# The even mixer's low halves shared with GpSimd, and five start times of steps, in a two-model fp32 block kernel

## The reference, cut to what matters

```python
aq, ak = rms_norm(a_q, qk_gains[0]), rms_norm(a_k, qk_gains[1])      # 8 heads of 64
logf = log_sigmoid(a_f + f_bias); cum_logf = cumsum(logf)
a_out = softmax(aq ak^T * scale + cum_logf_i - cum_logf_j, causal) av # forgetting attention
b_out = (softmax(q1 k1^T) - lam * softmax(q2 k2^T)) bv                # 4 differential heads
out = concat(a_out, rms_norm(b_out, gain)) @ w_out
# cross attention: k = rms_norm(mem_n @ w_k) per head of 256, v = mem_n @ w_v
```

## Time and profile before

| | |
|---|---|
| median of 3 runs | 1910.07 us (1909.57 to 1913.3) |
| the profiled execution | 1915.36 us, its span 1913.5 us |
| PE busy | 1885.3 us (99%) |
| DVE busy | 1301.3 us (68%) |
| ACT busy | 1119.2 us (58%) |
| POOL busy | 331.9 us (17%) |
| chain that ended last | PE 84%, DVE 7%, ACT 4%, DMA 3% |

### The profile page before, as it was taken

The page is one execution under the profiler, slowest core; times in us unless marked ns, Lnnn a source line. Parts: engine busy times, 40 slices in busy tenths (PEclk is TensorE's granted clock), DMA queues, the critical chain, the costliest instruction groups (busy, mean ns, idle before and its releaser), DMA issues.

```text
span 1913.5 us, 24906 instructions
## 1 busy us (share of the span) xinstructions
PE 1885.3 (99%) x9073; PEld 1627.2 (85%) x9073; DVE 1301.3 (68%) x1919; ACT 1119.2 (58%) x1685; POOL 331.9 (17%) x559
## 2 busy tenths in 40 slices
PE   8999999999999999999999899999999999999999
PEld 7888888888888888888887788888888887788888
DVE  6687776666876775666578766776666577856664
ACT  5586555555866654655467565654555466665552
POOL 1110123111101531022100000431122011101220
PEclk9999999999999999999999999999999999999999
DMA  8866699878657997698865354997788787746884
GB/s 268 255 204 186 203 256 295 261 223 255 201 182 221 281 286 230 184 263 254 236 183 177 121 187 135 288 278 231 229 256 255 227 256 229 211 138 194 253 254 143
DMA packets 283497, 429.97 MB, mean 225 GB/s; under 512 B 25028, under 2 KB 161440, under 8 KB 283120
## 3 DMA queue, kind: packets, MB, share of 16 engines
q1 hardware_dynamic: 256144, 352.41, 60.3%
q0 software_dynamic: 26768, 75.64, 14.6%
q10 hardware_dynamic: 464, 0.34, 0.1%
HBM read 393.15 MB, written 35.15 MB: 224 GB/s over the span
## 4 chain that ended last, share of the span: by engine, by line
PE 84%; DVE 7%; ACT 4%; DMA 3%; issue 2%; POOL 0%; ACTq 0%; DVEq 0%; POOLq 0%
PE M L954 26%; PE M L956 26%; PE M L955 26%; DVE WL L1478 3%; ACT WH L1216 1%; PE AUX L998 1%; PE AUX L1185 1%; PE AUX L1163 1%; DMA TG<-squares 1%; DMA squares<-TG 1%; DVE SM L1664 1%; ACT TMP L1251 1%; DVE TMP L1621 0%; DMA SQI<-squares 0%; DMA RAW<-in_w_in 0%
## 5 line engine op out<-in xcount | busy, mean ns | idle before, releaser
L1478 DVE TENSOR_TENSOR WL<-RAW,WH 128x1024 fp32r<-128x1024 f32 (+1 forms) x670 | 811.1, 1215 | 460.0 <-ACT WH L1216 457.4
L1216 ACT ACTIVATE WH<-RAW 128x1024 fp32r<-128x1024 f32 (+1 forms) x670 | 703.6, 1054 | 525.4 <-PE M L956 475.6
L954 PE MATMUL M<-WH,Bh 128*128 128x512 f32 x1792 | 689.2, 385 | 3.4 <-DVE WL L1478 2.0
L955 PE MATMUL M<-WL,Bh 128*128 128x512 f32 x1792 | 679.7, 379 | 0.0
L956 PE MATMUL M<-WH,Bl 128*128 128x512 f32 x1792 | 679.7, 379 | 0.0
L954 PEld LDWEIGHTS M<-WH,Bh 128*128 128x128 f32 x1792 | 339.1, 189 | 53.1 <-DVE WL L1478 4.4
L956 PEld LDWEIGHTS M<-WH,Bl 128*128 128x128 f32 x1792 | 339.0, 189 | 48.0
L955 PEld LDWEIGHTS M<-WL,Bh 128*128 128x128 f32 x1792 | 339.2, 189 | 45.6
L1246 ACT ACTIVATE AS<-M,KEEP 128x256 f32<-128x256 f32 x132 | 55.4, 470 | 78.0 <-PE M L956 78.0
L954 PE MATMUL M<-WH,MTh 128*128 128x512 f32 x128 | 54.5, 426 | 0.0
L1893 POOL TENSOR_TENSOR KEEP<-SM,KEEP 128x2 f32<-128x2 f32 x15 | 10.7, 711 | 240.2 <-DVE SM L1532 240.1
(11 more groups left out here) (473 smaller groups left out, 2746.0 us busy)
## 6 DMA issues: line engine op xcount, KB each, us to landing
RAW<-in_ffn_w_in SPq DMA_DIRECT2D x352, 256.0 KB, 3.9
RAW<-in_w_in SPq DMA_DIRECT2D x103, 512.0 KB, 4.8
RAW<-in_w_gate_up SPq DMA_DIRECT2D x176, 256.0 KB, 4.6
RAW<-in_ffn_w_out SPq DMA_DIRECT2D x88, 512.0 KB, 4.7
RAW<-in_w_down SPq DMA_DIRECT2D x44, 512.0 KB, 4.8
RAW<-in_x_w_kv SPq DMA_DIRECT2D x32, 512.0 KB, 4.2
RAW<-in_even_w_in SPq DMA_DIRECT2D x24, 512.0 KB, 4.4
RAW<-in_odd_w_in SPq DMA_DIRECT2D x24, 512.0 KB, 5.1
```

The source lines that it names most:

```text
L954: e.matmul(out, s.hi, wh, start=s.at0, stop=False)
L955: e.matmul(out, s.hi, wl, start=False, stop=False)
L1216: e.activation(p.WH[:, h, 0:s.size], p.RAW[:, i, 0:s.size], ACT.Copy).then_inc(k.w_hi, 1)
L1478: e.tensor_tensor(p.WL[:, h, 0:s.size], p.RAW[:, s.u % NRAW, 0:s.size], hi.bitcast(F32), ALU.subtract).then_inc(k.w_lo, 1)
```

## The change

Units 352, 355, ... 391 of the weights (number modulo 3 is 1, conversion planned while `crowded` is set, which is while the even mixer and the projections behind it are planned) get their low half from GpSimd, with a semaphore of their own, `w_spare`. TensorE and SyncE wait for the semaphore that belongs to the unit (`low_made`). Apart from that, due times change: of the squares and norm of the first X (`late`), of rsqrt, product and exchange of the memory keys' norms where they have `room` (+5.0; the keys of heads 2 and 3 in layer 0, all four heads' keys in layer 1), of the transposes of `ak` (6.9 to 6.2), of the first suffix sum and the first pair's output in each layer of the first model, and of the forgetting heads of the even mixer (start 0.4 to 1.3 behind av, 2.75 to 2.65 between heads). In `b` the third case is 6.4 either way, as before.

```diff
+        self.lows, self.spare, n = [], set(), [0, 0]
+        for s in [s for s in steps if s.kind == "conv"]:
+            n[s.spare] += 1
+            self.lows.append((s.spare, n[s.spare]))
...
+            v.spare = self.crowded and v.u % 3 == 1
...
-        late = 4.5 if source == "load" else 0.0
+        late = 2.0 if source == "load" else 0.0
...
-        r = self.rsqrt(c.end + 3.2, s.v, n, s)
-        f = self.add("hn", c.end + 3.8)
+        wait = 5.0 if room is not None and groups == 2 else 0.0
+        r = self.rsqrt(c.end + 3.2 + wait, s.v, n, s)
+        f = self.add("hn", c.end + 3.8 + wait)
...
-            self.heads_out(c.end + 7.0, c.end + 21.0, "hn", f, s.xs, *room, lab, form, dst, gain)
+            self.heads_out(c.end + 7.0 + wait, c.end + 21.0 + wait, "hn", f, s.xs, *room, lab, form, dst, gain)
...
-        b = (c.end + (6.9 if lab in ("aq", "ak") else 6.4), 1.0) if finish[3] is None else (c.end + 7.6, 2.5)
+        b = (c.end + (6.9 if lab == "aq" else 6.2 if lab == "ak" else 6.4 if n < 8 else 6.4), 1.0) if finish[3] is None else (c.end + 7.6, 2.5)
...
-                q = self.add("st_s", b + (4.9 if i else 6.1))
+                q = self.add("st_s", b + (4.9 if i else 6.6))
...
-            o = self.add("st_o", b + 8.5)
+            o = self.add("st_o", b + (8.5 if hp else 9.0))
...
-        self.heads(c.end + 0.4, 2.75, lab_o, ["aq0", "aq1", "ak0", "ak1"], VA, QA, KA, av, S["NB"], A, 0.0)
+        self.heads(c.end + 1.3, 2.65, lab_o, ["aq0", "aq1", "ak0", "ak1"], VA, QA, KA, av, S["NB"], A, 0.0)
...
+def low_made(k, u):
+
+    spare, n = k.p.lows[u]
+    return (k.w_spare if spare else k.w_lo), n
...
-                e.wait_ge(k.w_lo, s.u + 1)
+                e.wait_ge(*low_made(k, s.u))
...
+        if s.kind == "conv" and s.spare:
+            continue
...
+        elif s.kind == "conv" and s.spare:
+            h = s.u % NHL
+            e.wait_ge(k.w_hi, s.u + 1)
+            hi = p.WH[:, h, 0:s.size]
+            e.tensor_tensor(p.WL[:, h, 0:s.size], p.RAW[:, s.u % NRAW, 0:s.size], hi.bitcast(F32), ALU.subtract).then_inc(k.w_spare, 1)
...
-            e.wait_ge(k.w_lo, i - NRAW + 1)
+            e.wait_ge(*low_made(k, i - NRAW))
...
+            p.crowded = l == 0
...
+            p.crowded = False
```

More of the change, by code:

```diff
@@ L232, in __init__ @@
         self.n_unit = self.n_conv = 0
+        self.crowded = False
         self.bank_use = [0] * 4
@@ L273, in order @@
                 busy[b] = s.at + s.late + HELD.get(s.kind, 1.5)
+        self.lows, self.spare, n = [], set(), [0, 0]
+        for s in [s for s in steps if s.kind == "conv"]:
+            n[s.spare] += 1
+            self.lows.append((s.spare, n[s.spare]))
+            if s.spare:
+                self.spare.add(s.u)
         for i, s in enumerate([s for s in dve if s.kind == "bt"]):
@@ L875, in __init__ @@
         self.raw = [sem(f"raw{i}") for i in range(NRAW)]
-        self.w_hi, self.w_lo, self.w_used = sem("w_hi"), sem("w_lo"), sem("w_used")
+        self.w_hi, self.w_lo, self.w_spare, self.w_used = sem("w_hi"), sem("w_lo"), sem("w_spare"), sem("w_used")
         self.m_out = [sem(f"m_out{i}") for i in range(4)]
```

## The result

The changed kernel took **1924.86 us** (median of 4 runs, 1923.84 to 1927.92), the kernel before in the same rounds 1911.1 us (1909.57 to 1913.3): ratio 1.0075, interval 1.0063 to 1.0088. It is 14 us slower where 1903 was forecast. The profiled execution took 1927.92 us, span 1926.1. Ratios are of undisturbed executions: one of the six of experiment 11 took 3312.57 us at a granted clock of 0.557 and is left out of its ratio.

What follows compares the result with a forecast made beforehand. TensorE, busy 99% of the span, was taken as the bound. Terms -2.1 - 1.3 - 1.1 - 2.7 + 1.4 = -5.8 us, with 1.5 of 5.1 us slow clock, took the median 1910.07 to 1903 us; range 1898 to 1909.

Steps and rivals of the forecast that it cites:

- the step on the subtractions: 14 low halves on GpSimd, 2.4 us each, half lost on VectorE: 0 net, bounds -2.1 to +3.6 and 1.1 lost again.
- rival 2: VectorE is held for the whole of each subtraction: +3.6 us, 1.1 back, slow clock kept, 1909 us; chance 0.17.
- the sum of the due times: Gains of start, output, ak and memory keys: -2.1, -1.3, -1.1 and -2.7 us, plus 5.1 us of slow clock.
- Start: Squares and norm of the first X earlier: TensorE's wait for a low half near 34 us goes, -2.1 us.
- Suffix sums and output: First suffix sum moved, 0; first heads' output one step back fills its wait at 131 us, twice, -1.3 us.
- Key turn and forget scores: Even mixer near 1053 us: a 1.6 us wait replaces the 2.65 us KA wait, -1.1 us; 3.4 slow clock goes.
- the wait behind the BO norm: Even mixer at 1069.56 us: TensorE's 0.58 us wait behind this norm moves and stays.
- Norm of memory keys: Even mixer at 1100 us: TensorE's 3.0 us wait shrinks, -2.7 us and 1.7 of slow clock; odd mixer 0.
- Queue of GpSimd: Unit 361 behind the forget rows delays unit 365 and the KB copy near 1010 us: +1.4 us, bounds 0 to +3.
- Clock: One slow stretch left in the mixers, at 1640 us, instead of three; 5.1 us of slow clock goes, 1.5 counted.
- Rival 3: The stops only move; only start and output count, -3.4 + 1.4: 1908 us; chance 0.08.
- Rival 4: GpSimd becomes the even mixer's bound if a subtraction takes over 3.2 us: 1916 us at 4.0, about 1930 at 5.4; chance 0.08.

Runs made afterwards that it cites:

- experiment 11: The changed kernel again, unaltered, beside the kernel before: 1926.62 us median, ratio 1.0077.
- experiment 12: Kernel before with three edits: start's squares and norm earlier, key turn of ak earlier, memory keys' norm later in the even mixer only: 1904.41 us, ratio 0.9962.
- experiment 8: Changed kernel with unit 361's low half back on VectorE, 13 left on GpSimd: 1925.02 us, ratio 1.0067 to the kernel before.
- experiment 3: Kernel before with only the squares and norm of the first X due earlier (2.0 for 4.5): 1908.74 us, ratio 0.9983.
- experiment 6: Kernel before with only the first suffix sum (6.6) and first pair's output (9.0) later, in both layers: 1914.07 us, ratio 1.0014.
- experiment 5: Kernel before with only the memory keys' norms 5.0 later, in both mixers: 1911.12 us, ratio 0.9993.
- Experiment 10: Kernel before plus four GpSimd memsets of 128x512 into an idle tile at each of the 14 units: 1911.67 us, ratio 0.9996.
- experiment 2: Kernel before with only the 14 subtractions moved to GpSimd: 1924.43 us, ratio 1.0065.
- experiment 7: Kernel before plus two GpSimd subtractions of a constant tile (128x512) into an unread tile at each of the 14 units: 1919.09 us, ratio 1.0039.

## Why the prediction was wrong

**The step that failed** is the one on the subtractions: "I take half of its 2.4 us as lost on VectorE, which is what it saves: 0". Alone they cost 12.6 us. The length was right (2.37 us undisturbed). Two things in the step were wrong. A hold lasts to the end of the subtraction, 1.9 to 2.4 us in nine of eleven, not half of it, which is what rival 2 said. And the sum was made as a balance of VectorE's time, 1.22 saved against 1.2 or 2.4 lost, with only three of 14 counted. The two sides of that balance aren't the same goods. The saving lies on a low half that is made 8 to 16 us ahead of its use. The hold falls on whatever VectorE does at that moment, here products for which TensorE stands waiting. It should have been priced like this, an estimate: number of subtractions that start beside a head product, times 2 us, nothing off for the saving. The rows at hand didn't say how many have slack behind them, but 14 times 2 us less some slack would have put the far end of the range beyond +10, not at +3.6. Rival 2 had the mechanism, with a chance of 0.17 and a price of +3.6; it was 12.6.

**A second step failed beside it**: the sum of the due times, -7.2 us and 5.1 of slow clock. Without the subtractions it came to nothing (1911.58 us, ratio 1.0002), which is outside the range of 1898 to 1909 as well. The terms follow below.

The Trainium skill (SBUF — State Buffer, section on SBUF's two separate sides) says that whichever of the two engines starts first has the shared ports for its whole instruction, against VectorE instructions with two SBUF inputs or in a fast mode, the former only if GpSimd reads SBUF. The runs agree. A held instruction ends soon behind GpSimd's: up to 0.2 us for small ones, 0.55 for 128x512 and 1.1 for 128x1024, which is less than their own 0.68 and 1.22. In quarters it is held in quarters. By memsets those with two SBUF inputs aren't held at all, and two TENSOR_SCALARs are, up to the memset's end; that they are in a fast mode no trace shows. I had quoted it and given it 0.17, because no row of the kernel before showed it; a rule that speaks against the change deserved more.

**Start**: -2.1 forecast, -3.1 measured (interval -1.5 to -5.0), and the wait for WL gone. Right in mechanism, with luck in the size: the wait it was read from, 1.96 us, is 0.5 to 2.3 in other profiles. The power ended at 25.5 and not at 25.1:

```profile
24.82 0.72 POOL L1910 TENSOR_TENSOR KEEP<-SM,KEEP 128x2 f32<-128x2 f32 x1 [11.00 <-DVE SM L1549]
```

**Suffix sums and output**: -1.3 forecast, +2.7 measured. I said the second suffix sum "keeps its place and waits for the same VectorE product". The output was what stood between TensorE and the next pair's sum; moved behind it, it left that sum uncovered. I looked at the wait that it filled and not at the one that it had been filling.

**Key turn and forget scores**: at their own place -1.3 for the stop, as forecast (-1.1), and 3.1 of slow clock (3.4). The failed term is the wait behind the BO norm, which "moves and stays" at 0.58 us: it became 1.64, with more behind it. Net 0 in time (0.9998, interval 0.9989 to 1.0007). Experiment 12 shows the better half: the key turn without the scores' move wins 2.2 us at unit 373 beside the clock, and nothing comes back.

**Norm of memory keys**: -2.7 and 1.7 of clock forecast for the even mixer, -1.8 and 1.7 measured at the place, with a stop of 1.09 us left where under 0.5 was forecast; the 0 for the odd mixer was up to +1.2. I had looked at the copy that holds TensorE there and not at the keys' own use.

**Queue of GpSimd**: a wait for KB of 2.2 us near 1015 in the first profile (1.9 near 1010 forecast), none in the second. It takes turns with the head product behind it. The time of experiment 8 doesn't show a gain from its removal; its profile grows 1.1 to 2.2 us less lag than the changed kernel's two. The +1.4 fits that, but isn't shown.

**Clock**: not one slow stretch in the mixers but four (of 3.4, 6.8, 3.4 and 3.4 us, near 1015, 1073, 1104 and 1650 us). Those near 1073 and 1104 are at stops that the holds lengthened:

```profile
1073.40:1080.20 6.80, 6.02 (x20) 5.10 (x20) 2.87 (x12) 3.02 (x6) 0.00 (x0) 0.50 0.21 75
```

In all that is 17.0 us of slow clock where the kernel before had 13.6, so the clock is a small part of the loss. What was wrong in the prediction is the reading "5.1 of slow clock" as something that goes with its stop. The profiles show both outcomes for one and the same stop. The KA wait of 2.49 or 2.50 us is followed by 6.8 us of slow clock in the kernel before, by 3.4 in experiments 3 and 6, by none in 5 and 10; the 2.87 us wait of the earlier trace rows by 3.4 in the kernel before and experiment 3, by 6.8 in 10, by none in 6. Experiment 10, the KA wait and 6.8 us behind it:

```profile
1054.84 0.34 PE L1130 MATMUL AUX<-KA,QA 64*128 64x128 f32 x1 [2.49 <-ACT KA L1292]
...
1054.80:1061.60 6.80, 6.76 (x40) 5.82 (x41) 4.82 (x14) 3.76 (x15) 1.31 (x3) 1.00 0.34 115
```

Of what 5.1 us stand for, 3.1 and 1.7 us were there in the kernel before's profile, but an execution may be without them for no edit's sake. The forecast counted 1.5 of the 5.1 for the median, and even that isn't an edit's gain for sure.

Rival 3 (stops only move) holds for the four other edits together: 1911.6. Rival 4's time, 1916 and more, was near, for another reason: VectorE kept 29 us idle in 984 to 1118, so it never became the bound. TensorE was stopped by single late instructions, not by VectorE's sum. (The rival's arithmetic has a slip too: at 5.4 us a subtraction its own working gives about 1935, not 1930.)

**What stays open**: how the 12.6 us divide among the holds. In experiment 2 the lag grows at seven places up to unit 371, by 0.7 to 2.2 us each; behind them slow stretches come and go and mix with it, so a single hold's price wasn't read.

## What to carry to other kernels

Work moved to GpSimd isn't priced by VectorE's balance of busy time: look at which VectorE instruction would start beside each GpSimd instruction that reads SBUF, and charge its whole length there. Scalings of one tile (TENSOR_SCALAR) are held as well, reductions and instructions on PSUM weren't. If it must go to GpSimd, cut it: four pieces halved the loss. And when a stop is taken out, find the next product in line with its own margin before the gain is booked; only the retimings with a free stretch behind them (the start, ak, the even mixer's keys) kept their gain, and these three alone made the fastest kernel here. A slow stretch of the clock in one profile isn't a gain to be booked either: look at several profiles with the same stop.

## What the runs showed of the hardware

- The hold goes the other way too. At 1009.80 a subtraction took 3.27 us instead of 2.37, beside a VectorE instruction that had begun 0.18 us before it; and VectorE's three low halves took 5.83 us, where one takes 1.22:

```profile
1009.62 5.83 DVE L1495 TENSOR_TENSOR WL<-RAW,WH 128x1024 fp32r<-128x1024 f32 x3
1009.80 3.27 POOL L1915 TENSOR_TENSOR WL<-RAW,WH 128x1024 fp32r<-128x1024 f32 x1 [1.71 <-ACT WH L1231]
```

- It catches instructions with one tile and a number per partition as well (the TENSOR_SCALAR of 128x2: 2.25 us), and with one tile and constants (128x4: 1.48 us). A TENSOR_SCALAR is held by a memset too (0.71 us instead of 0.35), instructions on two SBUF tiles are not (36 of 36). None on PSUM was seen held, nor a TENSOR_REDUCE or RECIPROCAL of an SBUF tile.
- A wait of 2.5 us isn't always followed by the slow clock. In these 14 profiles slow stretches are seen by waits from 2.07 us (experiment 7, near 1050) on, and none by one of 3.61 us (experiment 6, near 75). The same wait for an ACT copy in the odd mixer, 2.52 us in both, left the clock at 0.50 in the kernel before and at 1.00 in experiment 12. For each, 3.4 us behind that wait:

The kernel before:

```profile
1640.10:1643.50 3.40, 3.40 (x9) 2.70 (x8) 3.40 (x6) 1.06 (x1) 0.00 (x0) 0.50 0.48 170
```

Experiment 12, with the wait itself:

```profile
1629.27 0.65 PE L1165 MATMUL AUX<-TMP,VD 128*64 128x256 f32 x4 [2.52 <-ACT TMP L1433]
...
1630.60:1634.00 3.40, 3.40 (x17) 2.98 (x16) 3.40 (x6) 1.45 (x2) 0.00 (x0) 1.00 0.47 160
```

That stretch is worth 1.66 us and comes and goes between executions of kernels that don't differ there: it is in 8 of the 14 profiles. The prediction counted on this stretch to stay.
